# Gate and up projections as seven block products, with the row scale behind the down projection

## The reference

```
x = x + merged @ w_out[i]
hn = rmsnorm(x, norm2_g[i])
gate, up = jnp.split(hn @ w_ffn_in[i], 2, axis=-1)
x = x + (jax.nn.silu(gate) * up) @ w_ffn_out[i]
```

## Time and profile before

| | |
|---|---|
| median of 3 runs | 2600.02 us (2596.5 to 2602.19) |
| span of the profiled execution | 2597.4 us |
| PE busy / weight loads busy | 2538.9 us (98%) / 2154.6 us (83%) |
| DVE / ACT / POOL busy | 1200.3 / 834.5 / 1159.6 us |
| read from HBM | 212.86 MB, 83 GB/s over the span |

### The profile page before, as it was taken

One profiled execution on the slowest core, in us unless ns is written; L12 is line 12 of the kernel. 1 busy time (PEld: TensorE's weight loads), 2 busy tenths in 40 slices (PEclk: granted clock), 3 DMA queues, 4 the chain that ended last, 5 costly groups with the idle time before them and its releaser, 6 DMA issues.

```text
span 2597.4 us, 37755 instructions
## 1 busy us (share of the span) xinstructions
PE 2538.9 (98%) x12947; PEld 2154.6 (83%) x12947; DVE 1200.3 (46%) x2275; ACT 834.5 (32%) x1473; POOL 1159.6 (45%) x586
## 2 busy tenths in 40 slices
PE   7999999999999999999999999999999999999998
PEld 6789988887888888899988888888899888888887
DVE  6567776664432221277775322211577765322211
ACT  4456655663211110144444211100244443211101
POOL 4335530000377788600000777788300002877885
PEclk8989989999999999999999999999999999999999
DMA  7321113332333333322232233333222222333332
GB/s 156 105 49 33 38 37 89 98 90 81 93 92 97 97 101 97 93 70 70 70 94 83 87 93 96 96 103 94 87 82 70 70 82 81 97 97 97 95 95 77
DMA packets 422189, 222.88 MB, mean 86 GB/s; under 512 B 59504, under 2 KB 420268, under 8 KB 422060
## 3 DMA queue, kind: packets, MB, share of 16 engines
q1 hardware_dynamic: 419100, 218.03, 29.6%
q10 hardware_dynamic: 2960, 3.22, 0.4%
HBM read 212.86 MB, written 2.10 MB: 83 GB/s over the span
## 4 chain that ended last, share of the span: by engine, by line
PE 88%; DVE 7%; ACT 3%; issue 2%; DMA 0%; DVEq 0%; ACTq 0%; POOL 0%
PE psA L1066 48%; PE psB L1089 13%; PE psA L1089 10%; PE psA L1322 5%; PE psB L1322 4%; PE psO L967 3%; PE psB L948 1%; PE psB L924 1%; DVE b L2013 1%; DVE b L2161 1%; DVE b L2053 0%; DVE b L1688 0%; DVE b L2034 0%; PE psO L1362 0%; DVE b L1672 0%
## 5 line engine op out<-in xcount | busy, mean ns | idle before, releaser
L1066 PE MATMUL psA<-b,b 128*128 128x512 f32 x5616 | 1288.0, 391 | 3.8 <-DVE b L1461 1.8
L1066 PEld LDWEIGHTS psA<-b,b 128*128 128x128 f32 x5616 | 1055.3, 188 | 234.5 <-issue 8.6
L743 POOL TENSOR_TENSOR b<-b,b 128x1024 fp32r<-128x1024 f32 x239 | 453.0, 1895 | 1202.5 <-PE psA L1066 1042.3
L745 POOL TENSOR_TENSOR b<-b,b 128x1024 fp32r<-128x1024 f32 x239 | 593.9, 2485 | 18.8
L1089 PE MATMUL psB<-b,b 128*128 128x512 f32 (+4 forms) x1626 | 367.3, 384 | 7.7 <-DVE b L1897 4.5
L1089 PEld LDWEIGHTS psB<-b,b 128*128 128x128 f32 (+2 forms) x1626 | 299.1, 195 | 68.1 <-DVE b L1897 4.9
L1089 PE MATMUL psA<-b,b 128*128 128x512 f32 x1356 | 324.4, 394 | 0.0
L1461 DVE SCALAR_TENSOR_TENSOR b<-psA,b 128x512 f32<-128x512 f32 x152 | 104.6, 690 | 461.6 <-PE psA L1066 457.7
L1089 PEld LDWEIGHTS psA<-b,b 128*128 128x128 f32 x1356 | 252.6, 188 | 54.4 <-issue 1.0
L1472 DVE TENSOR_TENSOR b<-b,psA 128x512 f32 x48 | 33.0, 688 | 337.9 <-PE psA L1066 337.9
L2347 ACT ACTIVATE b<-b,b (+1 forms) x56 | 40.6, 724 | 441.1 <-DVE b L1472 434.5
(11 more groups left out here) (271 smaller groups left out, 2177.2 us busy)
## 6 DMA issues: line engine op xcount, KB each, us to landing
b<-in_w_in SPq DMA_DIRECT2D x296, 256.0 KB, 3.0
b<-in_w_ffn_in SPq DMA_DIRECT2D x176, 256.0 KB, 3.1
b<-in_w_ffn_out SPq DMA_DIRECT2D x64, 256.0 KB, 3.0
b<-in_w_out SPq DMA_DIRECT2D x48, 256.0 KB, 3.0
b<-in_w_gate SPq DMA_DIRECT2D x44, 256.0 KB, 3.1
b<-in_w_up SPq DMA_DIRECT2D x44, 256.0 KB, 3.2
b<-in_w_down SPq DMA_DIRECT2D x32, 256.0 KB, 3.0
b<-in_w_ffn_out SPq DMA_DIRECT2D x32, 192.0 KB, 2.6
```

The costliest lines, as they stand in the source:

```text
L743: nc.gpsimd.tensor_tensor(w[:, 0], wraw[:, s], ones[:, 0:1].broadcast_to([P, KT * P]), ALU.mult).then_inc(w_hi.sem, 1)
L745: nc.gpsimd.tensor_tensor(w[:, 1], wraw[:, s], hi_f(w[:, 0]), ALU.subtract).then_inc(w_lo.sem, 1)
L1066: i = mm(dst, w[:, wh, kt * P:(kt + 1) * P], rhs(xh, kt), start=first and kt == 0 and n == 0, stop=last and kt == kts - 1 and n == 2)
```

## The change

The GU stage is cut into 11 quads: two gate tiles and two up tiles, 256 outputs each. With the weights' 8 row tiles taken as even and odd ones, A11 and A12 are the gate's even and odd parts, A21 and A22 the up's, each 4x2 tiles (128x1024). The activations are cut likewise: even and odd feature tiles, and the first and last 256 tokens. The 2x2 by 2x2 block product is made by Strassen's scheme (Winograd's form) with seven products: of the weights A11, S1 = A21 + A22, S2 = S1 - A11, S4 = A12 - S2, A12, A22 and S3 = A11 - A21 (`products_of`; A12 stands third in the first quad), and seven operands of the activations, half of which are differences. A product is 24 matmuls of 256 columns (L982), so a quad has 168 of them where it had 96 of 512 columns. Two products accumulate onto two others in PSUM; DVE makes the remaining sums.

- **Operands.** During WO, `even_operands` and `odd_operands` (ACT and DVE) replace `residual`'s split: for each pair of output tiles four differences of 128x256 on DVE (L2107, L2114, L2117, L2118), and high and low parts of seven operand pieces instead of four (ACT L2972, L2982, L2985; DVE L2110, L2120, L2125). WO chunks 2 to 7 are split by ACT (`out_hi`) and DVE (`out_lo`, L2129) instead of POOL.
- **Weights of a quad.** SP loads all 2 MB of a quad with four transfers of 512 KB into one of two buffers (`wraw2`, `wraw`), when the quad two before is split. POOL makes the four sums (L915, L918, L926, L927), the low parts of A12 and A22 (L936), and one sum of products (L948). ACT makes all seven high parts (L3009) and copies the other five weights into two banks of PSUM, `psS` (L3016), from which DVE subtracts the high part (L2144). Three slots take turns.
- **After the products.** ACT copies the first and fifth product from PSUM (L3022, L3028). DVE makes the sums (L2164, L2169, L2181, L2183, L2185) and scales the gate alone by -0.5 and `c_rs` (L2173, L2177); silu is one ACT instruction per quad (L3032), and DVE multiplies by the up tiles (L2190, L2193) into `hid_raw`.
- **The hidden tiles' parts** are no longer made as they come: the place of the high parts is taken by the quad buffers and operands until the last quad. ACT (L3040) and DVE (L2198) make them for all 11 pairs of tiles there.
- **Down.** ACT and DVE split the 24 chunks instead of POOL. The up factor's scale comes behind the down projection: DVE multiplies each output tile by -0.5 and `c_rs` (L2203) and then adds it to `xT` (L2205).

The core of the diff (lines are moved left by eight spaces):

```diff
...
+QUADS, SEVEN = FT // 2, 7
+A11, S1, S2, S4, A12, A22, S3 = range(SEVEN)
...
-    stage(c0 + 8, 2 * FT, lambda i, s: (up if s % 2 else gate)(i * 2 * P + (s // 2) * P))
-    stage(c0 + 8 + 2 * FT, 24, lambda i, s: down(s % 3 * KT, i * 4 * P + (s // 3) * P), per=12)
+    c1 = c0 + 8
...
+            sp.wait_ge(w_lo.sem, w_lo.at(c1 + place_of(q - 2, S3)))
+        settled(sp)
+        for x in range(2):
+            for b in range(2):
+                dst = quad_raw(q)[:, 2 * x + b, :].rearrange("p (j n) -> p j n", n=2 * P)
+                sp.dma_start(dst, quad(x, b, q)).then_inc(quad_in[q % 2], 16)
...
+        for q in range(QUADS):
+            sum_low(q)
+            if q == 0:
+                low(q, A12)
+            sum_high(q)
+            if q:
+                low(q, A12)
+            low(q, A22)
+            pool.wait_ge(fs_act.sem, fs_act.at(g + q, "fifth"))
+            settled(pool)
+            nc.gpsimd.tensor_tensor(fifth_product, fifth_product, first_product, ALU.add).then_inc(ff_pool.sem, 1)
...
-    proj(c0 + 8, t0 + 8, 0, ready=split_by(res_dve, n))
-    norm(k, n + 7)
-    proj(c0 + 9, t0 + 9, 1)
-    with pe.Fori(1, FT) as i:
-        for s in range(2):
-            proj(c0 + 8 + i * 2 + s, t0 + 8 + i * 2 + s, s)
...
+        for j in range(KT // 2):
+            for p in range(2):
+                at = (2 * j + p) * P
+                for m, (wh, xh) in enumerate(((0, 0), (0, 1), (1, 0))):
+                    i = nc.tensor.matmul(banks[x][:, p * half_t:(p + 1) * half_t], w[:, wh, at:at + P], rhs[x][:, xh, j, :],
+                                         start=first and j == 0 and p == 0 and m == 0,
+                                         stop=last and j == KT // 2 - 1 and p == 1 and m == 2, skip_group_check=True)
+        i.then_inc(used.sem, 1)
...
+            elif x == S2:
+                pe.wait_ge(res_dve.sem, res_dve.at(n + 7))
+            elif x == S4:
+                pe.wait_ge(fs_act.sem, fs_act.at(g + q, "fifth"))
+            elif x == A12:
+                if q == 0:
+                    norm(k, n + 7)
+                    pe.wait_ge(xo_dve.sem, xo_dve.at(x0 + 3, "lo_low"))
+                pe.wait_ge(fs_act.sem, fs_act.at(g + q, "first"))
+            elif x == A22 and q:
+                pe.wait_ge(fs_dve.sem, fs_dve.at(g + (q - 1), "h1"))
+            elif x == S3:
+                pe.wait_ge(fs_dve.sem, fs_dve.at(g + q, "u2"))
+            product(q, x)
...
+            def pairs(kt):
+                if kt % 2 == 0:
+                    pe.wait_ge(fl_dve.sem, fl_dve.at(g + (q * KT + kt) // 2))
+
+            chunk(c2 + i * 6 + s, s, psA[:, m, :], lambda h, kt: hid[:, 1 - h, q * KT + kt, :], rows, q == 0, q == 2,
+                  ready=pairs if first else None, slot=slots2[s % 3])
...
+            v.tensor_tensor(w[:, 1], psS[:, :, :].rearrange("p b t -> p (b t)"), hi_f(w[:, 0]), ALU.subtract).then_inc(w_lo.sem, 1)
...
+        def down_residual(m):
+            s = m % 2
+            dve.wait_ge(used.sem, used.at(c2 + (3 * m + 2)))
+            v.scalar_tensor_tensor(psA[:, s, :], psA[:, s, :], -0.5, c_rs[:, :], ALU.mult, ALU.mult).then_inc(dn_dve.sem, 1)
+            dve.wait_ge(dn_dve.sem, dn_dve.at(d0 + m))
+            v.tensor_tensor(xT[:, m, :], xT[:, m, :], psA[:, s, :], ALU.add).then_inc(drained.sem, 1)
+            residual(n + 8 + m, m, s, gain1(m), None)
...
+        for j in range(KT // 2):
+            added(2 * j)
+            for w in out_ahead.get(2 * j, []):
+                out_lo(w)
+            even_operands(j)
+            squares_added(2 * j)
+            if j == 3:
+                lo(0, A11)
+                lo(0, S1)
+            added(2 * j + 1)
+            for w in out_ahead.get(2 * j + 1, []):
+                out_lo(w)
+            odd_operands(j)
+            squares_added(2 * j + 1)
+            odd_lo(j)
+        lo(0, S2)
+        lo(0, S4)
...
+        middle_sum(0)
+        lo(0, S3)
+        gate_high(0)
+        gate_low(0)
+        lo(1, A11)
+        lo(1, S1)
+        for q in range(1, QUADS):
+            up(q - 1)
+            product_high(q - 1)
+            lo(q, S2)
+            product_low(q - 1)
+            lo(q, S4)
+            middle_sum(q)
+            gate_high(q)
+            lo(q, S3)
+            gate_low(q)
+            if q < QUADS - 1:
+                lo(q + 1, A11)
+                lo(q + 1, S1)
+        q = QUADS - 1
+        down_lo(0)
+        for i in range(4):
+            hidden_lo(i)
+        down_lo(1)
+        up(q)
+        product_high(q)
+        product_low(q)
+        for i in range(4, 6):
+            hidden_lo(i)
+        down_lo(2)
+        for i in range(6, QUADS):
+            hidden_lo(i)
+        for m in range(KT):
+            if m < KT - 1:
+                down_lo(3 * m + 3)
+                down_lo(3 * m + 4)
+                down_lo(3 * m + 5)
+            down_residual(m)
...
+            act.wait_ge(used.sem, used.at(c1 + (c - 3)))
+            raw = quad_raw(q)
+            src = {A11: raw[:, 0], S1: sum1, A12: raw[:, 1], S4: sum1, S2: sum2, A22: raw[:, 3], S3: raw[:, 2]}[x]
+            ac(quad_slot(c)[:, 0], src[:, :], ACT.Copy).then_inc(w_hi.sem, 1)
+            if x in (A12, A22):
+                return
+            if x != A11:
+                act.wait_ge(w_lo.sem, w_lo.at(c1 + place_of(q, {S1: A11, S2: S1, S4: S2, S3: S4}[x])))
+            elif q:
+                act.wait_ge(w_lo.sem, w_lo.at(c1 + place_of(q - 1, S3)))
+            ac(psS[:, :, :].rearrange("p b t -> p (b t)"), src[:, :], ACT.Copy).then_inc(wc_act.sem, 1)
...
+            even_operands(j)
+            if j == 3:
+                hi(0)
+                hi(1)
+                hi(2)
+            for w in out_ahead.get(2 * j + 1, []):
+                out_hi(w)
+            odd_operands(j)
+        for q in range(QUADS):
+            c = SEVEN * q
+            if q:
+                hi(c + 2)
+            first(q)
+            hi(c + 3)
+            fifth(q)
+            hi(c + 4)
+            if q == 0:
+                norm(k)
+                nc.scalar.preload_act_table_set("silu_and_others")
+            hi(c + 5)
+            hi(c + 6)
+            hi(c + 7)
+            if q == QUADS - 1:
+                down_hi(0)
+                hidden_hi(0)
+                hidden_hi(1)
+            hi(c + 8)
+            silu(q)
+        hidden_hi(2)
+        hidden_hi(3)
+        down_hi(1)
+        hidden_hi(4)
+        hidden_hi(5)
+        down_hi(2)
...
```

400 lines of the change are left out of this document (308 added, 92 removed).

## The result

The changed kernel takes 2582.8 us (median of four, 2580.5 to 2585.0) where the kernel before takes 2598.8: a ratio of 0.9937, 95% interval 0.9921 to 0.9953. So it is 0.5 to 0.6% faster, where 2607.5 us, 0.3% slower, was forecast. The time lies in the range given, but the sign was wrong: the kernel was forecast to become slower and became faster.

The account below looks back on a forecast made before the run. PE was taken as the bound, so only its matmul stream and gaps count. Per tail -18.9 + 13.9 + 4.0 + 0.7 + 1.5 + 1.3 = +2.5 us, three times +7.5, giving 2607.5 us; range 2578 to 2632.

Parts of the forecast that it names:

- What the products save: GU's matmul stream: 1848 matmuls at 120.0 ns, 221.8 us instead of 240.7, saving 18.9 us per tail.
- DVE and POOL block each other: With two SBUF inputs each, one waits for the other's whole instruction; with one DVE input from PSUM this doesn't happen.
- Steady quads: Quads within GU: a ring of steps that doesn't pass PE takes 19.6 us, fits PE's 20.16, so priced at nothing.
- Start of GU: First quad after WO: 11.5 us lost, plus 2.8 from WO, less 0.4 of before: 13.9 us per tail.
- Clock: PE's clock partly at 1.2 GHz after new gaps of 6.1, 4.0 and 3.0 us: 1.5 us per tail.
- register waits: The start's 38 handovers take 0.05 us more in two of three tails: 1.3 us per tail on average.
- the path over ACT to A22: First quad: after the norm's matmul, ACT's norm steps from 18.4 to 23.0, A22's low part at 26.6; PE waits 4.0 us.
- The collision in WO: POOL's S1 and S2 fall into WO and push the operand work back by 2.8 us.
- The turns with S4 and S3: Start of GU: DVE's differences take turns with POOL's instructions; 11.5 us lost, against 6.1 without any blocking.
- End of GU: Last quad into down: PE waits 3.0 us for the fifth hidden pair, 1.0 between pairs 5 and 6; 4.0 per tail.
- Scale behind down: After down: hidden under matmuls except after the last tile, 0.7 us per tail.
- Overlap at the start holds: Faster rival, chance 0.24: DVE and POOL hardly meet at GU's start; 2575 us, some 2587 if only WO is undisturbed.

Follow-up runs that it names:

- e1: Changed kernel without ACT's five weight copies into PSUM per quad, DVE's low parts reading weights straight from SBUF: 2671.7 us, ratio 1.0281 to the kernel before.
- e8: Changed kernel with one more POOL sum of 2.4 us per quad, ahead of S1: 2623.4 us, ratio 1.0089 to the kernel before.
- c1: The changed kernel built again unaltered and timed beside three of the experiments: 2586.5 us, ratio 0.9954 to the kernel before.
- e10: Changed kernel with 30 unread matmuls of 256 columns ahead of the wait for the norm: 2589.5 us, ratio 0.9967 to the kernel before.
- e12: Changed kernel with POOL's S1 and S2 of the first quad cut to 16 columns in the two layers (output wrong): 2580.0 us, ratio 0.9927.
- e13: Changed kernel with POOL's S4 and S3 of the first quad cut to 16 columns in the two layers (output wrong): 2577.3 us, ratio 0.9924.
- e14: Changed kernel with all four POOL sums of the first quad cut to 16 columns in the two layers: 2573.1 us, ratio 0.9901.
- e7: Changed kernel with hidden pairs 4 and 5 made ahead of the last quad's sums, 6 and 7 ahead of the third down weight: 2585.6 us, ratio 0.9949.
- e6: Changed kernel without the multiplication of each down tile by -0.5 and c_rs (output wrong): 2586.5 us, ratio 0.9948 to the kernel before.
- e4: Changed kernel with e2's edit, A22's first-quad high part ahead of the norm's steps, and the norm's matmul awaiting only the squares: 2579.3 us, ratio 0.9927.
- e2: Changed kernel with POOL starting A12's first-quad low part only after DVE's last four differences: 2580.6 us, ratio 0.9930 to the kernel before.

## Why the prediction was wrong, step by step

**What bounds the kernel**: right. PE is the bound in both kernels, and all of the result is the length of its stream and the waits in it.

**What the products save**: right, 0.6 us low. 1848 matmuls at 119.05 ns are 220.0 us for 221.8. In the trace before, 240.9 to 241.0 us pass from WO's end to the down projection, and less the norm's 0.87 and a wait of 0.4 to 0.6 the 44 chunks took 239.5, 5.44 each: 19.5 saved per tail, not 18.9. The rule of the Trainium skill (TensorE: Matmul & The Clock Gate, Back-to-back issue gap), 109 ns for 256 columns, would give 201.8 us by the prediction's estimate. The trace doesn't agree: the quads' stream runs at 118.9 ns, with 1513 weight loads to 1514 matmuls; whether these are the reason, no run here shows. The measurement decides for the row, as the prediction had it.

**DVE and POOL block each other**: right, and the heart of the matter (e1). The rule of the Trainium skill (SBUF — State Buffer, Who interferes with whom), that a DVE instruction with at most one SBUF input doesn't contend with POOL and one with two does, is borne out: 165 instructions of 1223 ns with an input from PSUM, 2297 ns from SBUF.

**Steady quads**: right at nothing. The ring is estimated at 18.6 us, not 19.6 (e8).

**Start of GU**: here the sum failed. It gave 11.5 and 2.8, and clock and register waits on top, 17.1 in all. G less 220.9 is 11.7 us in the first tail (11.0 in c1) and 12.7 in the layers. Two steps failed: two terms were put on top that were already in it, and the path over ACT to A22 was summed too long. In the layers, with times after WO's end and the prediction's with its 2.8 added:

- **Clock, 1.5, and register waits, 1.3, were added to a loss that already held them.** The end of the start is set by A22's low part: the 20.9 us of PE's own work have 15.2 ahead of A22, and A22's matmuls began at 27.7, which makes 12.5 of the 12.7. What PE loses ahead of that is hidden, though only just: PE is there no more than 0.1 to 0.6 us early, so that neither loss can be won back alone. The slow clock behind A11 and behind the norm cost nothing (e10, and the two layers above), and the gaps of 4.0 and 3.0 us, for which the 1.5 stood, never came: the profile has 0.6, 0 and 0.55 at A22 and 1.7 at the fifth pair. PE came to A22 later than summed, at 27.2 to 27.6 and not 25.3, for its 48 matmuls behind the norm ran 1.3 to 1.8 us long. Of registers the trace has some 0.1 us per handover between first tail and layers (the gap ahead of L2114 is 0.98 and 1.07 us, ahead of L2125 0.19 and 0.28), but the 11.8 us of the next point are the same in all three tails, so hardly any of it reaches the end there; ahead of it the share stays open.
- **The path over ACT to A22 was too long.** The norm's matmul came at 15.9, for 15.8 predicted. From there to the end of A22's low part the prediction has 13.6 us (13.0 to 26.6). It is 11.8 in the three tails of the changed kernel and 11.7 to 11.8 in the layers of e12, e13 and e14. ACT began the norm's steps 3.4 us after the norm's matmul and not 5.4, being done sooner with the high parts and copies of S2 and S4; the rest of the path, 8.4, is as summed (8.2). So A22's low part ended at 27.7 and not at 29.4, in the first tail at 26.6.
- The collision in WO: 2.8 summed; it moves the norm's matmul by 3.0 and G by 2.4 to 3.0 (e12, and e13 against e14).
- The turns with S4 and S3 behind the first: 5.4 summed (11.5 less 6.1). They move the norm's matmul by 4.1 to 4.7 and A22's low part by 4.1 (e12 against e14), but G by 2.6 to 3.2 only. For without them PE waits 2.07 us for A22 and runs its 24 matmuls 1.5 us slow, and with them it comes there late and waits 0.1 to 0.4, at full clock.
- Without blocking: 6.1 summed, 7.1 measured (e14), with that 1.5 of clock in it.

The start was too dear by 17.1 less 12.4 on average, 4.7 us per tail: 2.8 for clock and registers, 1.9 in the chain.

**End of GU**: 4.0 summed, bounds 3 to 5; 1.9 to 2.0 measured. The place is right, the fifth pair. DVE began the last quad's sums at 958.8, only 2.8 us after the first down matmul, and made the fifth pair by 7.3 us after it, not 8.4; the wait between pairs 5 and 6 was 0.3 and not 1.0. And the order matters less than thought (e7). The whole stretch from the first down matmul to what follows the tail is 2.9 to 3.2 us longer than before, where 4.7 was summed with the scale; 0.5 to 0.6 of that is in no wait and stays open.

**Scale behind down**: right, 0.6 for 0.7 (e6).

The forecast of +2.5 us per tail stands against -4.7, -4.2 and -4.1, a difference of 6.8: 4.7 at the start, 0.6 in the stream and 0.2 of rounding make 5.5 between WO and down, 1.6 lie behind it, less 0.3 by which WO became longer (44.1 to 44.3 us for 43.8 to 44.0). Three times 6.8 is 20.4 of the 24.7 us between 2607.5 and 2582.8; the parts between the tails, which the change doesn't touch, were 2.4 us shorter in this profiled execution, and the rest lies in the medians. Of the rivals, "Overlap at the start holds" comes nearest in time (2575, or 2587 if only WO is undisturbed) and is wrong in its mechanism. It was to be decided by whether the third difference ends nearer to 7 or 12 us after WO; it ends at 12.5 in the first tail and 13.4 in the layers, so DVE and POOL do meet, as forecast. What hid was PE's loss, not the turns. That 2582.8 still lies within the range is owed to the range's width and not to the mechanism.

## What to carry to other kernels

Where several chains run side by side from one point (here the norm, the operands and A22's low part), write down when each ends and take the latest; a wait, the slow clock behind it and the next wait can be one loss and not three (e10), while the clock behind the last wait is paid (e4, e14). Price clock and handovers only where the sum has not already counted the time in which they fall. And where DVE works beside POOL, try to move one input of its longer steps to PSUM even at the price of a copy on another engine: a microsecond of copying per step kept 85 to 89 us out of this kernel (e1).

## What the runs showed of the hardware that was not expected

- The turns hurt both sides. Without the PSUM copies not only DVE's low parts went from 1223 to 2297 ns; POOL's S1 went from 2422 to 3320 ns, with no change of its own (e1).
- After a short wait the granted clock may fall or not. A11's 24 matmuls took 3.11 us after 2.36 us of waiting in the first tail of the changed kernel (granted clock 1.00) and 4.41 after 2.35 in e4's (0.65); 3.10 after 2.93 in e6's (1.00) and 4.61 after 2.95 in e2's (0.63). In the layers of the changed kernel it is 4.54 and 5.49 after 3.2 (0.64 and 0.50). The shortest wait with a fall behind it is that for A22 in e10, 2.06 us (4.62, 0.63). Matmuls that nobody reads, put into the gap, kept the clock at 1.00 in two tails of three (e10), and no time was won by it.
- The first 720 us, alike in all kernels, differ by up to 8 us between profiled executions. The end of a change of 0.5% is better read from stretches of the trace than from two medians.
